# Moving weight splits later and two-part running sums in a two-block transformer kernel on one core

## The reference

```python
z = jnp.einsum('bqhd,bshd->bhqs', q_blk, k).astype(jnp.float32) * (HEAD_DIM ** -0.5)
strict = dist > 0
log_keep = jnp.where(strict, jax.nn.log_sigmoid(-z), 0.0)
log_between = lax.cumsum(log_keep, axis=3, reverse=True) - log_keep
a = jnp.where(strict, jnp.exp(jax.nn.log_sigmoid(z) + log_between), 0.0)
...
h = a * jax.nn.sigmoid(g)
h = jnp.pad(h, ((0, 0), (CONV_KERNEL - 1, 0), (0, 0)))
h = lax.conv_general_dilated(
    h, dw_w[:, None, :].astype(h.dtype), window_strides=(1,), padding='VALID',
    dimension_numbers=('NWC', 'WIO', 'NWC'), feature_group_count=CONV_WIDTH)
```

## Time and profile before

| What | Value |
|---|---|
| median of three executions | 773.2 us |
| the profiled execution, its own time | 773.35 us |
| its span, first to last instruction | 771.5 us |
| TensorE matmuls busy | 760.8 us, 99% of the span |
| VectorE busy | 582.8 us, 76% |
| ScalarE busy | 408.6 us, 53% |
| granted TensorE clock, mean | 1.00 |
| chain that ended last | PE 85%, VectorE 8%, DMA 3%, ScalarE 2% |

### The profile page before, as it was taken

One profiled execution on the slowest core, in us unless ns is written; L12 is line 12 of the kernel. 1 busy time (PEld: TensorE's weight loads), 2 busy tenths in 40 slices (PEclk: granted clock), 3 DMA queues, 4 the chain that ended last, 5 costly groups with the idle time before them and its releaser, 6 DMA issues.

```text
span 771.5 us, 9633 instructions
## 1 busy us (share of the span) xinstructions
PE 760.8 (99%) x3712; PEld 636.2 (82%) x3712; DVE 582.8 (76%) x945; ACT 408.6 (53%) x555; POOL 49.3 (6%) x42
## 2 busy tenths in 40 slices
PE   8989999999999999999999999999999999999998
PEld 6878899888888888888888887888988888888886
DVE  5698688697757878687778838699857777768584
ACT  7666255456657546545454546764665344353430
POOL 0200000000001500000000005041000000000000
PEclk9999999999999999999999999999999999999999
DMA  9953434454544467665665567655133665655601
GB/s 334 391 175 110 136 110 142 159 168 161 163 164 164 159 204 249 192 216 175 208 205 179 173 207 273 218 172 164 56 110 109 222 215 181 200 184 199 206 13 54
DMA packets 68508, 137.28 MB, mean 178 GB/s; under 512 B 2544, under 2 KB 6256, under 8 KB 67824
## 3 DMA queue, kind: packets, MB, share of 16 engines
q1 hardware_dynamic: 68032, 135.30, 52.6%
q10 hardware_dynamic: 432, 1.38, 0.5%
HBM read 135.48 MB, written 1.05 MB: 177 GB/s over the span
## 4 chain that ended last, share of the span: by engine, by line
PE 85%; DVE 8%; DMA 3%; ACT 2%; SPq 1%; issue 1%; ACTq 0%
PE b L652 19%; PE b L654 18%; PE b L653 18%; PE SS L652 4%; PE SS L654 4%; PE SS L653 4%; DVE wlo L1605 2%; PE TT L621 2%; PE OO L652 2%; PE OO L654 2%; PE OO L653 2%; DMA cs<-in_cst 2%; DVE ca L2128 2%; DMA xr<-in_x 1%; PE b L814 1%; PE SS L761 1%
## 5 line engine op out<-in xcount | busy, mean ns | idle before, releaser
L1605 DVE TENSOR_TENSOR wlo<-raw,whi 128x2048 fp32r<-128x2048 f32 (+2 forms) x119 | 269.9, 2270 | 80.3 <-ACT whi L1144 79.5
L1144 ACT CAST whi<-raw 128x2048 fp32r<-128x2048 f32 (+2 forms) x119 | 222.9, 1878 | 124.4 <-PE b L654 81.9
L652 PE MATMUL b<-whi,Ahi 128*128 128x512 f32 (+2 forms) x520 | 206.7, 398 | 2.9 <-ACT gates L1217 2.4
L654 PE MATMUL b<-whi,Alo 128*128 128x512 f32 (+2 forms) x520 | 199.8, 384 | 0.0
L653 PE MATMUL b<-wlo,Ahi 128*128 128x512 f32 (+2 forms) x520 | 199.1, 383 | 0.0
L652 PEld LDWEIGHTS b<-whi,Ahi 128*128 128x128 f32 x520 | 97.8, 188 | 21.1 <-ACT gates L1217 2.9
L654 PEld LDWEIGHTS b<-whi,Alo 128*128 128x128 f32 x520 | 97.6, 188 | 19.9
L653 PEld LDWEIGHTS b<-wlo,Ahi 128*128 128x128 f32 x520 | 97.9, 188 | 17.8
L1993 DVE STREAM_TRANSPOSE hT<-ust 32x256 f32<-32x256 f32 (+1 forms) x192 | 81.5, 425 | 2.8
L652 PE MATMUL b<-whi,Bhi 128*128 128x512 f32 x154 | 60.5, 393 | 0.1
L654 PE MATMUL b<-whi,Blo 128*128 128x512 f32 x154 | 60.0, 390 | 0.0
(11 more groups left out here) (295 smaller groups left out, 1095.1 us busy)
## 6 DMA issues: line engine op xcount, KB each, us to landing
raw<-in_w_in SPq DMA_DIRECT2D x38, 1024.0 KB, 5.1
raw<-in_w_up SPq DMA_DIRECT2D x16, 1024.0 KB, 5.4
raw<-in_w_dn SPq DMA_DIRECT2D x16, 1024.0 KB, 5.1
raw<-in_w_d SPq DMA_DIRECT2D x11, 1024.0 KB, 5.0
raw<-in_w_g SPq DMA_DIRECT2D x10, 1024.0 KB, 5.0
raw<-in_w_u SPq DMA_DIRECT2D x10, 1024.0 KB, 5.1
raw<-in_w_out SPq DMA_DIRECT2D x8, 1024.0 KB, 5.1
raw<-in_w_br SPq DMA_DIRECT2D x4, 1024.0 KB, 5.0
```

Source lines behind the costliest of these rows:

```text
L652: e.matmul(dst, xh, H[:, kc, c0:ce], start=first and kc == krs[0], stop=False)
L654: ins = e.matmul(dst, xl, H[:, kc, c0:ce], start=False, stop=last and kc == krs[-1])
L1144: e.copy(whi[:, s, 0:m], raw[:, r, 0:m]).then_inc(s_hi, 1)
L1605: e.tensor_tensor(wlo[:, s, 0:m], raw[:, r, 0:m], whi[:, s, 0:m].bitcast(F32), ALU.subtract).then_inc(s_lo, 1)
```

## The change

Five edits:

1. **Splits.** From unit 86 to unit 97 the place of the split is put later: unit 86 from group 174 to 175, unit 87 from 176 to 180, unit 88 from 178 to 182, unit 89 from 180 to 184, unit 90 from 182 to 185, unit 91 from 184 to 187, and so on, to one group later at unit 97. Units 87, 88 and 89 now stand two groups ahead of their first use (groups 182, 184 and 186), unit 90 three.
2. **Running sums.** Instead of one fp32 matmul of 384 columns with `LG`, there are two fp32r ones, with the high and the low half of `L`. ScalarE makes the high half and, once, an fp32r copy of `LG` (`sh`); VectorE makes the low half (`sd`). The 128-column product with `UO` stays in fp32.
3. **Heads** start at slots 8, 10, 14, 16 and have the new step at +3.
4. **Taps.** 4, 6, 5 and 5 in place of 2, 4, 3 and 3 at slots 12, 14, 16 and 18; 4 a round in place of 6 in the first four rounds of attention.
5. **Masks.** `MB`, `UO`, `LG` (768 columns) are loaded ahead of unit 7, the rest behind it as before.

```diff
-    for h, a in enumerate((8, 9, 14, 15)):
-        for k, name in ((0, "sz"), (1, "sm"), (2, "ss"), (4, "sc"), (5, "su"), (6, "sp"), (7, "so")):
+    for h, a in enumerate((8, 10, 14, 16)):
+        for k, name in ((0, "sz"), (1, "sm"), (2, "ss"), (3, "sh"), (4, "sc"), (5, "su"), (6, "sp"), (7, "so")):
             bg[a + k].append((name, h))
...
-    for s, n in ((10, 8), (12, 2), (14, 4), (16, 3), (18, 3)):
+    for s, n in ((10, 8), (12, 4), (14, 6), (16, 5), (18, 5)):
         bg[s].append(("cv", n))
...
         if g >= turn:
             g = free_at[i - NSPL]
+        first = min(groups[t] for t in unit_of if unit_of[t] == i)
+        if i >= unit_of["p2", 4, 1, 0]:
+            g = max(g, first - {unit_of["p2", 4, 1, 0]: 6, unit_of["wo2", 0, 0, 0]: 5}.get(i, 2))
+            if i > unit_of["wo2", 1, 1, 0]:
+                g = max(free_at[i - NSPL], first - 3 - max(0, i - unit_of["u", 0, 0, 0]) // 2)
         g = max([g] + [h + 1 for h in split_after])
+        assert g <= first - 2, (i, g, first)
         split_after[g] = i
...
         for i in range(NRAW, nu):
+            if i == NRAW + 3:
+                o = CST["MB"][0]
+                e.dma_start(cs1[:, o:N1], cst_d[:, N0 + o:N0 + N1]).then_inc(d_cs0, 16)
             if i == NRAW + 4:
                 e.dma_start(cst[:, 136:N0], cst_d[:, 136:N0]).then_inc(d_cs1, 16)
-                e.dma_start(cs1[:], cst_d[:, N0:N0 + N1]).then_inc(d_cs1, 16)
+                e.dma_start(cs1[:, 0:CST["MB"][0]], cst_d[:, N0:N0 + CST["MB"][0]]).then_inc(d_cs1, 16)
...
         def sc(h, s):
...
-            w.wait_ge(d_cs1, 32)
+            w.wait_ge(d_cs0, 16)
             w.wait_ge(s_ss, h + 1)
+            w.wait_ge(s_lg, 1)
             clear(bk)
             R, L = bank[bk], Sb[:, h % 2, 384:768]
-            e.matmul(R[:, 0:384], c1("LG"), L, start=True, stop=False)
+            Lh, Ll = sum_split(h)
+            w.wait_ge(s_sh, h + 1)
+            e.matmul(R[:, 0:384], LGr[:], Lh, start=True, stop=False)
+            w.wait_ge(s_sd, h + 1)
+            e.matmul(R[:, 0:384], LGr[:], Ll, start=False, stop=False)
             e.matmul(R[:, 128:256], c1("UO", 128, 128), L[:, 256:384], start=False, stop=True).then_inc(s_sc, 1)
...
+        def sh(h):
+            if h == 0:
+                w.wait_ge(d_cs0, 16)
+                e.copy(LGr[:], c1("LG")).then_inc(s_lg, 1)
+            w.wait_ge(s_ss, h + 1)
+            w.wait_ge(s_sc, h - 1)
+            e.copy(sum_split(h)[0], Sb[:, h % 2, 384:768]).then_inc(s_sh, 1)
...
+        def sd(h):
+            Lh, Ll = sum_split(h)
+            w.wait_ge(s_sh, h + 1)
+            e.tensor_tensor(Ll, Sb[:, h % 2, 384:768], Lh.bitcast(F32), ALU.subtract).then_inc(s_sd, 1)
...
-            conv(6 if k < 4 else 4 if k < 8 else 1)
+            conv(4 if k < 8 else 1)
```

More of the change, by code:

```diff
@@ L207, in build @@
         gap = ExitStack()
+        with ExitStack() as r5:
+            LGr = sb("LGr", [128, 128], F32R, c=r5)
         gates = sb("gates", [128, 2, 4096], c=gap)
@@ L212, in build @@
         Sb = sb("Sb", [128, 2, 768], c=r1)
+        with ExitStack() as r5:
+            LH = sb("LH", [128, 2, 768], F32R, c=r5)
         PT = sb("PT", [128, 2, 768], c=r1)
@@ L253, in build @@
     d_xt = [sem(f"d_xt{i}") for i in range(5)]
+    d_cs0 = sem("d_cs0")
     d_x0, d_x1, d_par, d_cst, d_cs1, d_par2, d_tw, d_tw3, d_hp, d_out = [
@@ L286, in build @@
     s_pool = sem("s_pool_step")
+    s_lg, s_sh, s_sd = sem("s_lg_round"), sem("s_sb_soft_hi"), sem("s_sb_soft_lo")
     s_warm = sem("s_warm")
@@ L424, in build, with sum_split @@
                                          + [("N3", t, n) for t, n in ORD])}
+    def sum_split(h):
+        return LH[:, h % 2, 0:384], LH[:, h % 2, 384:768]
     nsq = nlf[:].rearrange("p t x -> p (t x)")
@@ L1280, in stages1 @@
                     sm(i)
+                elif name == "sh":
+                    sh(i)
                 elif name == "su":
@@ L1856, in stages1 @@
                     ss(i)
+                elif name == "sh":
+                    sd(i)
                 elif name == "su":
```

## The result

The changed kernel takes **780.6 us** (median of four runs, 780.4 to 781.0) against 773.4 us before on the same chip (773.1 to 773.9): a ratio of 1.0093, 95% interval 1.0075 to 1.011. That is slower by 7.2 us, 0.9%. The forecast was 774.9 us, the range 772.4 to 777.0 us. The sign was right, the size was not, and the time lies above the range. Times of kernels are medians that leave out one execution far off the others (845.1 us, clock 0.85, of the kernel with both unit 86 and the taps put back).

What follows compares the result with a forecast made beforehand. The prediction took TensorE as the bound. From 773.35 us, masks and heads -2.2, running sums -1.2, taps and splits around attention +1.3 and splits inside the output projection +3.65 gave 774.9 us, range 772.4 to 777.0 us.

Steps and rivals of the forecast that it cites:

- What bounds the kernel: Whole kernel: TensorE, busy 760.8 of 771.5 us, is the bound; only its work or its stops can change the time.
- Masks and heads: At the head: earlier masks replace TensorE's stop of 2.6 us at group 12 by one of 0.4 us, -2.2 us.
- sums: Running sums of four heads: two fp32r matmuls of 0.17 us replace one fp32 matmul of 0.64 us, -1.2 us.
- the head gives half back: Rival at the head: copy-outs in chunks 3 and 4 come late, gain -1.2 instead of -2.2, 776.0 us; chance 0.2.
- Taps and splits around attention: Around attention: six taps ahead of `r1` lengthen TensorE's stop by 2.4 us, attention gives back 1.1 us, net +1.3 us.
- Splits inside the output projection: Output projection: TensorE waits 3.35 us at group 186 for unit 89's split, 0.3 us for unit 90's, +3.65 us.
- The clock: Rival: behind each of two long stops the clock falls to 1.2 GHz, 1.6 us each, 776.5 to 778.0 us; chance 0.1.
- The last of the prediction's own signs of being wrong: At either long stop: a clock row below 1.00 under it would show the forecast wrong.
- The stop at group 186 does not come: Rival in the output projection: VectorE splits unit 89 before TensorE ends group 185, nothing lost there, 771.3 us; chance 0.08.
- Attention follows VectorE: Rival in attention: four rounds that lose two taps each get 0.8 us shorter, -1.1 instead of +1.3, 772.5 us; chance 0.12.

Runs made afterwards that it cites:

- experiment 3: Two kernels: the changed kernel with the old splits and taps, 770.7 us; the old kernel with only the late splits and moved taps, 783.0 us (trace meant here).
- the second measurement: The changed kernel run once more, unaltered: 778.9 us.
- experiment 5: The changed kernel with unit 89 split behind group 183 in place of group 184, all other splits unmoved: 775.6 us.
- the first combined version: The change's head and sums; units 86, 87, 88 late, unit 89 behind group 183, later ones when a slot is free, three taps moved into attention: 773.4 us.
- experiment 2: The changed kernel with nine matmuls at its very start in place of six: 779.1 us.

## Why the prediction was right or wrong

**What bounds the kernel: right.** Every microsecond of the result is a stop of TensorE, a slow stretch of it, or work taken from it.

**Masks and heads -2.2, sums -1.2: right in size, -3.4 forecast.** From the start to 209 us the changed kernel won 3.6 us, once the +2.0 us at the start is taken off. The two new matmuls of a head stand 0.17 us apart, as worked out from the rows of 260 columns:

```profile
45.39 0.33 PE L751 MATMUL TT<-LH,LGr 128*128 128x384 f32 x1
45.56 0.34 PE L753 MATMUL TT<-LH,LGr 128*128 128x384 f32 x1
```

VectorE no longer waits for `cs`, and PE has no wait for a copy-out at group 13, so that *the head gives half back* fell. **But the step missed what the stop at group 12 was worth as a cover.** The profiled run of before had a good start, so I counted 2.6 us of stop as winnable in every run. In the one trace that has the old head and a slow start (experiment 3) none of it is left. The start is a term of 2.0 us that no part of my sum held, and the trace of before could not have shown it. The loads came as counted: the masks were in at 30.8 us in this trace.

**Taps and splits around attention +1.3: the net was right, +2.4 and -1.1 both measured.** The cause was incomplete. I wrote that none of the splits ahead of `r1` is gone and left unit 86's move by one group at nothing on ScalarE. It alone costs 1.6 us, and only because the taps cost more did that not show. It mattered as soon as the taps were put back.

**Splits inside the output projection +3.65: right.** The stop came where the rows of the old kernel put it: from the transposes to group 186 it is now 586.44 - 582.70 = 3.74 us and was 581.73 - 581.38 = 0.35, so 3.4 us more, against 3.35. Behind it units 90 and 91 cost 1.0 us (the shift from 586 us to the end is 2.55 us, of which 1.5 is the clock) against 0.3. Unit 91, whose split stands behind group 187, has a wait of 0.43 us of its own at group 190; I had counted room there. Term: 4.4 us, just above its bound of 4.3.

**The clock: the step that failed.** I had the mechanism, its place and its price (1.6 us for each stop; 1.5 measured) and gave it 0.1. The price was right by luck: I took six matmuls at 0.26 us each, and it was eight at 0.2. I argued from a stop of 2.43 us that left the clock at 1.00, and treated two stops half as long again as if they were like it. The Trainium skill, "TensorE: Matmul & The Clock Gate", section "HAM oscillation", warned of this; the trace now agrees, with a clock of 0.55 to 0.59 behind both. The last of the prediction's own signs of being wrong, a clock row below 1.00 under a stop, is what came. This rival should have been the forecast: 774.9 + 3.0 = 777.9 us. With 0.7 us more for units 90 and 91 and 2.0 us for a slow start the sum is 780.6. The clock is the deciding part of the three: the second measurement, whose trace has a good start, took 778.9 us, still above the range, and with the two slow stretches taken off, 3.1 us, it would lie inside.

**The other rivals.** *The stop at group 186 does not come*: fell, 3.1 us of wait; it would have needed one group more of lead (experiment 5). *Attention follows VectorE*: fell, VectorE waits 6.3 us for the scores, in three waits.

## What to carry to other kernels

Cost a stop of TensorE that is longer than any in the trace at its length and the slow stretch behind it, and try first whether idle matmuls in it win that stretch back. Before counting a stop as a gain, ask what varies ahead of it: it may be absorbing that, and its removal then brings the scatter into the total. When work is moved off one engine's path, look at the other engine that does the other half of it (here the copy of unit 86 on ScalarE), for two late causes of one wait show as one.

## What the runs showed of the hardware

- PE idle for 1.1, 2.4 and 2.7 us left the clock at 1.00 in the traces. Behind idle times of 3.1 to 3.5 us matmuls of 512 columns stood 0.43 us apart, seven to eleven of them, at 12 of 13 such places in eight traces. The thirteenth is a surprise: in the run with the taps put back TensorE waited 3.14 us at group 186 and went on at full clock, although the same place was slow in six other traces:

```profile
582.00:584.00 2.00, 0.00 (x0) 0.00 (x0) 2.00 (x2) 1.96 (x2) 0.00 (x0) 1.00 0.00 0
584.00:586.00 2.00, 1.74 (x8) 1.44 (x9) 0.81 (x2) 1.09 (x3) 0.00 (x0) 1.00 0.33 37
586.00:588.00 2.00, 2.00 (x12) 1.69 (x11) 0.68 (x2) 0.00 (x0) 0.00 (x0) 1.00 0.96 341
```

Two of that kernel's four executions, the traced one among them, have a mean clock of 0.999, two of 0.995 and 0.996. So the fall is likely there, not certain. Where it comes, it cost 1.5 us behind most stops and 2.5 us in the trace with eleven slow matmuls.
- The waits of 2.3 to 2.7 us may not be safe either, and no trace settles it. Kernels with two slow stretches have mean clocks of 0.996 or less, those with one 0.997 or 0.998. So the two executions at 0.995 and 0.996 just named lost more than one usual stretch, although that kernel has one stop of over 3 us. And one execution of the first combined version, whose longest stop is 2.3 us in the trace, has 0.997 and took 775.7 us, 2.3 us above the median.
- At the start of the program the clock row does not show it: in the changed kernel the stretch from 6 to 8 us reads 1.00, with matmuls 0.43 us apart. The trace's record of the clock has its first entry there at 9.53 us, and the row counts what lies ahead of it as 1.00.

```profile
5.93 1.19 PE L688 MATMUL SS<-whi,Ahi 128*128 128x512 f32 x2 [1.70 <-ACT whi L1175]
6.92 1.05 PE L691 MATMUL SS<-whi,Alo 128*128 128x512 f32 x2
7.78 1.06 PE L694 MATMUL SS<-wlo,Ahi 128*128 128x512 f32 x2
```

- Why the first piece of weights lands 0.4 to 0.6 us later in some runs, and why equal waits are followed by slow matmuls in one run and by fast ones in another, stays open. That nine matmuls take the scatter away rests on one kernel with five executions, and experiment 2 doesn't show it.
